# Final normalization of a decoder trunk tile by tile, with odd tiles' products on DVE and even tiles' on ACT and Pool

## The reference

```
def rms_norm(x, w):
    xf = x.astype(jnp.float32)
    y = xf * lax.rsqrt(jnp.mean(xf * xf, axis=-1, keepdims=True) + EPS)
    return (y * w.astype(jnp.float32)).astype(x.dtype)
...
    yb = lax.map(expert_block, (xb, blk_expert)).reshape(n_rows, d)
    out = jnp.zeros_like(xt).at[row_tok].add(yb * row_w[:, None].astype(yb.dtype))
...
        x = x + hier_moe(h, w_coarse[i], b_coarse[i], w_fine[i], b_fine[i], w_gate[i], w_up[i], w_down[i])
    return rms_norm(x, final_norm)
```

## Time and profile before

| | us |
| --- | --- |
| three runs: lowest, median, highest | 1501.02, 1502.64, 1502.64 |
| profiled execution, its time | 1498.86 |
| profiled execution, its span | 1497.0 |
| TensorE busy in the span | 1372.8 (92%) |
| DVE busy | 977.4 (65%) |
| ACT busy | 786.8 (53%) |
| Pool busy | 554.7 (37%) |

### The profile page before, as it was taken

One profiled execution on the slowest core, in us unless ns is written; L12 is line 12 of the kernel. 1 busy time (PEld: TensorE's weight loads), 2 busy tenths in 40 slices (PEclk: granted clock), 3 DMA queues, 4 the chain that ended last, 5 costly groups with the idle time before them and its releaser, 6 DMA issues.

```text
span 1497.0 us, 19671 instructions
## 1 busy us (share of the span) xinstructions
PE 1372.8 (92%) x6510; PEld 1131.8 (76%) x6510; DVE 977.4 (65%) x918; ACT 786.8 (53%) x845; POOL 554.7 (37%) x485
## 2 busy tenths in 40 slices
PE   7999999999999999899992599999999999999950
PEld 5888888888888787688782478888888888888740
DVE  5433433575555758800326388999999998998857
ACT  5342214355434546200132178888888888888844
POOL 2444444766555666948003112211221112112112
PEclk9999999999999999999995699999999999999985
DMA  4112112233322244514214189999999999999756
GB/s 168 55 48 78 49 49 87 75 107 109 102 88 80 73 131 155 176 52 163 108 57 154 54 298 396 383 379 378 376 376 379 383 391 382 395 383 390 269 205 267
DMA packets 99540, 308.68 MB, mean 206 GB/s; under 512 B 15648, under 2 KB 17568, under 8 KB 99360
## 3 DMA queue, kind: packets, MB, share of 16 engines
q1 hardware_dynamic: 89840, 291.17, 53.5%
q0 software_dynamic: 9648, 16.80, 3.0%
HBM read 293.62 MB, written 32.64 MB: 218 GB/s over the span
## 4 chain that ended last, share of the span: by engine, by line
PE 82%; DVE 8%; POOL 3%; ACT 2%; DMA 2%; issue 1%; SPq 0%; DVEq 0%; ACTq 0%; POOLq 0%
PE ps L843 34%; PE ps L558 28%; PE ps L719 9%; PE ps L832 2%; DVE X L1594 2%; PE ps L665 2%; PE ps L674 2%; POOL M L1663 1%; PE ps L795 1%; DMA ring_dn<-in_moe 1%; PE ps L863 1%; POOL GH L1638 1%; PE ps L652 1%; POOL GL L1640 1%; PE ps L645 1%
## 5 line engine op out<-in xcount | busy, mean ns | idle before, releaser
L1638 POOL TENSOR_TENSOR GH<-raw,ones 128x512 fp32r<-128x512 f32 x106 | 132.9, 1254 | 293.6 <-PE ps L558 253.8
L558 PE MATMUL ps<-XH,GH 128*128 128x512 f32 x656 | 206.7, 394 | 0.4 <-DVE T L1334 0.4
L558 PE MATMUL ps<-XL,GH 128*128 128x512 f32 x656 | 203.7, 390 | 0.0
L558 PE MATMUL ps<-XH,GL 128*128 128x512 f32 x656 | 203.4, 389 | 0.0
L1640 POOL TENSOR_TENSOR GL<-raw,GH 128x512 fp32r<-128x512 f32 x106 | 156.6, 1477 | 8.3
L1535 DVE TENSOR_TENSOR split_c<-ring_gu,split_c 128x1024 fp32r<-128x1024 f32 x127 | 149.7, 1219 | 1.1 <-ACT split_c L1083 1.1
L558 PEld LDWEIGHTS ps<-XH,GL 128*128 128x128 f32 x656 | 123.1, 188 | 26.0
L558 PEld LDWEIGHTS ps<-XL,GH 128*128 128x128 f32 x656 | 123.2, 188 | 25.8
L558 PEld LDWEIGHTS ps<-XH,GH 128*128 128x128 f32 x656 | 121.3, 188 | 26.7 <-issue 1.7
L843 PE MATMUL ps<-split_c,XTH 128*128 128x512 f32 x520 | 139.8, 391 | 0.0
L1083 ACT ACTIVATE split_c<-ring_gu 128x1024 fp32r<-128x1024 f32 x130 | 130.1, 1049 | 1.6 <-PE ps L843 1.0
(11 more groups left out here) (285 smaller groups left out, 2872.8 us busy)
## 6 DMA issues: line engine op xcount, KB each, us to landing
ring_gu<-in_moe SPq DMA_DIRECT2D x264, 512.0 KB, 5.8
ring_dn<-in_moe SPq DMA_DIRECT2D x132, 512.0 KB, 6.7
raw<-in_win SPq DMA_DIRECT2D x82, 256.0 KB, 2.7
T<-acs_d SPq DMA_DIRECT2D x16, 512.0 KB, 5.3
raw<-in_wout SPq DMA_DIRECT2D x32, 256.0 KB, 2.7
T<-in_x SPq DMA_DIRECT2D x8, 512.0 KB, 7.3
X<-in_x SPq DMA_DIRECT2D x8, 512.0 KB, 4.4
h_d<-M SPq DMA_DIRECT2D x8, 512.0 KB, 2.6
```

Source lines behind the costliest of these rows:

```text
L558: mm = pe.matmul(ps[:, bank + h, :], wp[:, w, col], x[:, kk, h * 512:(h + 1) * 512], start=(kk == 0 and n == 0), stop=(kk == KT - 1 and n ...
L1638: link(pool, pool.tensor_tensor(hi, raw[:, r, :], one.to_broadcast([P, GR]), ALU.mult), g_hi, at + 1)
```

## The change

The roots, reciprocals and products of the last normalization are no longer made for four tiles at once. ACT makes a root (128x1) for every tile right behind its square. DVE makes a reciprocal for every tile, one tile behind its sums: that of tile `t - 1` comes after the sums of tile `t`. The products are divided by parity instead of by half: for odd tiles DVE makes the one-instruction product right behind the reciprocal, for even tiles ACT's scaled Copy (behind the root of the odd tile that follows) and Pool's product. SP takes the outputs in the order of tiles as before, and waits for `o_early` and `o_ready` in turn.

```
             for t in range(TT):
-                if t < TT // 2:
-                    sp.wait_ge(o_early, t + 1)
-                else:
-                    sp.wait_ge(o_ready, t - TT // 2 + 1)
+                sp.wait_ge(o_ready if t % 2 else o_early, t // 2 + 1)
                 sp.dma_start(a["out"][t], X2[:, t, :]).then_inc(out_done, 16)
...
                 act.wait_ge(x3_ready, t + 1)
                 st.link(act.activation(FSQ, X2[:, t, :], ACT.Square,
                                        accum_out=stat[:, 4, t:t + 1]))
-                if t % 4 == 3:
-                    half = slice(t - 3, t + 1)
-                    link(act, act.activation(stat[:, 5, half], stat[:, 4, half], ACT.Sqrt,
-                                             bias=eps[:, 0:1], scale=1.0 / D), dev3, t // 4 + 1)
-                if t == 3:
-                    act.wait_ge(inv3, 1)
-                if 3 <= t < 7:
-                    act.activation(X2[:, t - 3, :], X2[:, t - 3, :], ACT.Copy,
-                                   scale=stat[:, 6, t - 3:t - 2]).then_inc(scaled, 1)
+                act.activation(stat[:, 5, t:t + 1], stat[:, 4, t:t + 1], ACT.Sqrt,
+                               bias=eps[:, 0:1], scale=1.0 / D).then_inc(dev3, 1)
+                if t % 2 == 1:
+                    act.wait_ge(inv3, t)
+                    act.activation(X2[:, t - 1, :], X2[:, t - 1, :], ACT.Copy,
+                                   scale=stat[:, 6, t - 1:t]).then_inc(scaled, 1)
...
-                if t == 3 or t == TT - 1:
-                    half = slice(t - 3, t + 1)
-                    dve.wait_ge(dev3, t // 4 + 1)
-                    link(dve, dve.reciprocal(stat[:, 6, half], stat[:, 5, half]), inv3,
-                         t // 4 + 1)
-            for t in range(TT // 2, TT):
-                dve.scalar_tensor_tensor(X2[:, t, :], X2[:, t, :], stat[:, 6, t:t + 1],
-                                         nrow[:, D:2 * D], ALU.mult, ALU.mult
-                                         ).then_inc(o_ready, 1)
+                for n in [t - 1] * (t >= 1) + [t] * (t == TT - 1):
+                    one = slice(n, n + 1)
+                    dve.wait_ge(dev3, n + 1)
+                    link(dve, dve.reciprocal(stat[:, 6, one], stat[:, 5, one]), inv3, n + 1)
+                    if n % 2:
+                        dve.scalar_tensor_tensor(X2[:, n, :], X2[:, n, :], stat[:, 6, one],
+                                                 nrow[:, D:2 * D], ALU.mult, ALU.mult
+                                                 ).then_inc(o_ready, 1)
...
-            for t in range(TT // 2):
-                pool.wait_ge(scaled, t + 1)
+            for t in range(0, TT, 2):
+                pool.wait_ge(scaled, t // 2 + 1)
                 pool.tensor_tensor(X2[:, t, :], X2[:, t, :], nrow[:, D:2 * D], ALU.mult
                                    ).then_inc(o_early, 1)
```

## The result

The changed kernel took 1504.26 us in the median of 22 runs (1501.81 to 1507.23), the kernel before 1501.73 us in 22 runs beside them (1498.29 to 1503.75). The ratio is 1.0017 with a 95% interval of 1.0010 to 1.0023: slower by 2.5 us (1.5 to 3.5). That is within 0.2%, as forecast, though the interval reaches 0.23%. The time lies in the range; the shift is 2.5 us where I had 0.9.

What follows compares the result with a forecast made beforehand. DVE bounds a 40.3 us tail: sums, reciprocals, products and Pool's holding end the last sum 1.8 us later at 1488.35; the span ends at 1497.9, 0.9 us more, giving a median of 1503.5, range 1500.0 to 1505.8.

Steps and rivals of the forecast that it cites:

- The path up to the last sum: DVE's chain of sums, reciprocals and products in the tail: tile 7's sums end at 1488.35, 1.8 us later than before.
- the wait for the first root: DVE ahead of tile 0's reciprocal: waits only 0.2 to 0.25 us, since tile 1's sums cover the table load.
- the three held products: DVE's products of tiles 1, 3 and 5 each held 1.9 to 2.05 us by a Pool product, 5.95 in all.
- The exclusion: In the tail a Pool product and a DVE instruction of this shape don't run together; whichever comes second waits.
- From the last sum to the end: Tile 7's root and product, Pool's product of tile 6, then two outputs: from 1488.35 to the end at 1497.9.
- end at 1497.9: Program's close: last output lands at 1497.5 and the span ends at 1497.9, 0.9 us more than before.
- the prediction's own sign of being wrong: Stretch ahead of the tail: the prediction is wrong if the time before 1456.7 moves by more than a microsecond.
- The 1503.5: Forecast median of the whole kernel: 0.9 us added to the three runs' median of 1502.64.
- A late first root: Rival at DVE's first reciprocal: tile 1's sums cover nothing, 2.6 us more, end 1500.5, 3.5 us slower; chance 0.12.
- a drain of 1.38 us behind the load: Case at ACT's table load: the page's drain makes the term 1.9 instead of 0.5, end 1499.3; chance 0.04.
- No exclusion: Rival: DVE's products 1, 3 and 5 run beside Pool's in 1.3 us, not 3.2; 3.1 us faster; chance 0.08.
- Products going ahead of Pool: Rival: DVE's product goes first and Pool waits; 0.6 us later in all, end 1498.5; included in the forecast's 0.76.

Runs made afterwards that it cites:

- Two other kernels: The kernel before with a 128x1 Pool instruction behind DVE's last product, ratio 1.0023; the changed kernel with tile 6's product moved to DVE, ratio 0.9976.
- the two with all products on DVE: The changed kernel with all eight products on DVE, ratio to before 0.9972; the same with ACT's table load ahead of the first sums, 0.9970.
- the kernel with the small instruction: The kernel before with one Pool instruction of 128x1 elements added behind DVE's last product; ratio to before 1.0023, 3.5 us slower.

## Why the prediction was right, and where it was not

**The path up to the last sum** held. Forecast: it ends 31.6 us after the first sum starts (1488.35 less 1456.8). Measured: 31.2. The wait for the first root was 0.25 us (forecast 0.2 to 0.25), no later reciprocal of the sums' part waited, and the three held products took 3.18 to 3.23 us, 1.9 to 1.95 held each, 5.8 in all instead of 5.95. The rest of the 0.4 is in overlaps of a tenth each. That Pool's product is what holds them is shown by the kernel without it.

**The exclusion** was read rightly from two sums and one product of the kernel before. The Trainium skill (SBUF — State Buffer, "Who interferes with whom") states it: a DVE instruction with two inputs in SBUF contends with a GpSimd instruction that reads SBUF. It calls the ports that the two share an exclusive lock, and says that issue order decides who blocks. The trace agrees: 3.2 us beside Pool and 1.29 without, while a reciprocal of one input is not held. On who goes first one pair stands apart: the DVE sum at 1477.29 has its recorded start 0.01 us ahead of Pool's, and was the one held. I did not draw the consequence that the kernel with all products on DVE shows: holding costs DVE 1.95 us for each Pool product, and the product itself costs it 1.2, so dividing these products between the two engines loses time wherever they meet.

**From the last sum to the end** is where the size was off. Forecast: 9.55 us (1488.35 to 1497.9). Measured: 11.1 (1488.9 to 1500.0). Up to the last landing the steps held: tile 6's product on Pool ends at 1494.2, 5.3 us after the last sum (forecast 1493.6, 5.25); the outputs leave 0.4 us apart; the last lands 9.3 us after the last sum (forecast 9.15, 1497.5). The term that failed is the last one, "end at 1497.9", the 0.4 us from landing to end, taken over from the kernel before. I took the last landing as what closes the program. In this kernel it closes 5.8 us after Pool's last instruction, and that was 1.4 us later than landing plus 0.4. The prediction had put Pool's last product at 1493.6, and 5.8 us behind that is 1499.4, not 1497.9. Two other kernels show the same: 5.8 after a Pool instruction of 0.19 us, and 0.4 after landing again once Pool's last product is early. The kernel before hid it: 1494.6 against 1497.0, 2.4 us to spare.

The tail so grew by 2.0 us instead of 0.9. Against the kernel before, the last sum ends 1.4 us later (31.2 us after the first sum instead of 29.8), from there to the last landing it is 0.8 shorter (9.3 instead of 10.1), and from the landing to the end 1.4 longer. The runs say 2.5 with an interval that holds 2.0. The part ahead of the tail, which is the same in both, varies by 3.6 us from one profiled execution to the next, so the remaining 0.5 is left to it; that was not shown for the medians. By the prediction's own sign of being wrong, that part should not move by more than a microsecond: it moved by 1.02 in the two traces, so the sign was drawn tighter than the scatter of single executions allows.

**The time itself** came out closer than the working deserves. The 1503.5 stands on a median of three runs, 1502.6; the 22 runs of the kernel before have 1501.7. A start 0.9 us too high and a shift 1.6 us too small left the forecast 0.8 us below the 1504.3 measured. That is partly luck.

**The rivals.** A late first root did not come: 0.25 us of waiting. The rule of the Trainium skill (ScalarE: Activation LUTs, "What ACT_TABLE_LOAD costs") on a drain of 1.38 us behind the load is not borne out: the root starts 0.01 us behind the load's end (1461.59 + 1.28 = 1462.87, to 1462.88), and taking the load away from the path gave back 0.3 to 0.4 us. No exclusion: refuted. Products going ahead of Pool: among the sums Pool went first each time, by 0.2 to 0.5 us. The forecast was right in verdict because all terms were small beside 3 us, not because every one was known; the missing 1.4 us would have carried the change over 0.2% had the sums come out 1 us later.

## What to carry to other kernels

When work of this shape is divided between DVE and Pool, count what each Pool instruction holds on DVE, not only what it takes off: here 1.95 us held for 1.2 us of work. With eight products on DVE alone the tail is 3.0 us shorter than with four and four divided by half, and 7.1 shorter than with four and four divided by parity. At the end of a program ask of each engine, not only of the last transfer, when it finishes: Pool's last instruction should end 5.4 us or more before the last output lands (5.8 less the 0.4 that follows the landing anyway). A tail is best compared from a common start (here the first sum), since the identical part ahead of it moved by more than the change.

## What was not expected of the hardware

The program ends 5.8 us after Pool's last instruction has ended, whether that is a product of 128x1024 (2.67 us) or an instruction on 128x1 (0.19 us), as long as the last output has landed by then. The views above leave out what Pool does in this time, but the recorded traces hold it: each engine has an instruction named DRAIN under line 124, behind all its work. Pool's ends at 1499.81 in the changed kernel, 5.57 us after its last product, and Pool then releases the other engines. In the kernel before it ends at 1494.37, likewise 5.57 us after Pool's last product, and the outputs are still under way. In the kernel without Pool's products and in the two with all products on DVE it starts 1.7 us after Pool's last scatter, with nothing of Pool's work under way, and takes 5.54 us; it takes the same 5.54 us in the kernel with the small instruction, 0.07 us behind that instruction's end. So it is a time of its own that follows Pool's work, and not a part of the work. Why it takes so long no run shows. DVE has no such time: in the kernel with all products on DVE its DRAIN ends 0.05 us after its last product, at 1489.57, and the span ends at 1492.6, 0.4 us after the last output has landed.
